# Two-layer hybrid trunk on eight cores: heads prepared evenly between the attention steps, and the output projection of the context block run inside the last pair of heads

## What is computed

```
u, cq_raw, ckv, krope = ab_split(h, w_in, kv_norm_g)
q = rms_norm(rms_norm(cq_raw) @ w_uq)            # 8 heads of 96, latent queries rotated
kv = ckv @ w_ukv                                 # k_nope 64 and v 64 per head
k = rms_norm(concat(k_nope, krope)); v
y_att = softmax(q k^T * 96**-0.5) v              # context: own 256 keys; latent: 512 cached + 1024 own
y = concat(y_pool, y_att) @ w_out                # 1024 x 1024
x = x + gate * y                                 # gate, shift, scale from silu(cond) @ ada_w + ada_b
x = x + gate2 * swiglu(norm(x))
```

## Time and profile before

| | |
|---|---|
| median of three runs | 1262.86 us |
| lowest, highest | 1261.05, 1441.05 us |
| profiled execution | 1259.46 us, span of its slowest core (5) 1258.4 us |
| spans of the eight cores | 1248.7 to 1258.4 us |
| mean granted clock of the cores | 0.955 to 0.972 |
| TensorE, VectorE, ScalarE, GpSimd busy | 90%, 38%, 34%, 18% of the span |
| preparation of pair 0 with pooling | 136.3 to 166.5 us |
| attention, four pairs | 166.5 to 359.6 us |
| output projection, to the first FFN matmul | 359.6 to 405.4 us |

### The profile page before, as it was taken

The page is one execution under the profiler, slowest core; times in us unless marked ns, Lnnn a source line. Parts: engine busy times, 40 slices in busy tenths (PEclk is TensorE's granted clock), DMA queues, the critical chain, the costliest instruction groups (busy, mean ns, idle before and its releaser), DMA issues.

```text
span 1258.4 us, 17871 instructions; the slowest of 8 cores (1248.7 to 1258.4 us)
## 1 busy us (share of the span) xinstructions
PE 1137.0 (90%) x6857; PEld 547.9 (44%) x6857; DVE 480.3 (38%) x814; ACT 429.5 (34%) x669; POOL 227.8 (18%) x347
## 2 busy tenths in 40 slices
PE   2477678797889899999999999998899999999998
PEld 1233455554544344444444444444344444444443
DVE  0355673634136211152252253565622225125133
ACT  2455466665745511101101156543651110110100
POOL 3311452533213200000000022224310000000000
PEclk9988997868799899999999999998999999999999
DMA  9960318778991425225224206003533321410013
GB/s 187 239 110 1 59 30 141 112 118 130 155 167 36 67 38 92 39 35 84 34 34 84 51 1 109 1 1 49 98 55 67 68 35 34 84 17 1 1 76 126
DMA packets 24977, 90.04 MB, mean 72 GB/s; under 512 B 3392, under 2 KB 3776, under 8 KB 24128
## 3 DMA queue, kind: packets, MB, share of 16 engines
q0 software_dynamic: 21312, 77.10, 36.8%
q1 hardware_dynamic: 3584, 11.80, 2.8%
HBM read 153.85 MB, written 6.88 MB: 128 GB/s over the span
## 4 chain that ended last, share of the span: by engine, by line
PE 76%; DVE 7%; DMA 6%; ACT 5%; POOL 3%; issue 3%; POOLq 0%; ACTq 0%; DVEq 0%
PE pb L230 74%; DMA wslot<-w_in_u 3%; DMA wslot<-ada_w 3%; ACT pt L247 2%; DVE xtmp L268 2%; PE pb L228 2%; DVE kT L274 1%; POOL qs L251 1%; DVE xb L268 1%; DVE qf L274 1%; POOL qr L251 1%; ACT hy L247 0%; ACT xsq L247 0%; POOL qt L251 0%; DVE utok L251 0%
## 5 line engine op out<-in xcount | busy, mean ns | idle before, releaser
L230 PE MATMUL pb<-hb,wslotx 128*128 128x512 bf16 x1440 | 319.9, 379 | 0.0
L247 ACT ACTIVATE sg<-pb 128x512 f32<-128x512 f32 x132 | 78.7, 596 | 472.0 <-PE pb L230 472.0
L251 DVE TENSOR_TENSOR apart<-pb,sg 128x512 bf16<-128x512 f32 x132 | 91.3, 691 | 369.0 <-PE pb L230 346.2
L230 PEld LDWEIGHTS pb<-hb,wslotx 128*128 128x128 bf16 x1440 | 140.8, 98 | 170.0 <-issue 0.3
L268 DVE SCALAR_TENSOR_TENSOR xb<-pb,mod,xb 128x512 f32<-128x512 f32 x192 | 143.6, 749 | 143.1 <-PE pb L230 143.1
L230 PE MATMUL pb<-hb,wslot 128*128 128x512 bf16 x864 | 197.6, 385 | 0.0
L230 PE MATMUL pb<-apart,wslot 128*128 128x512 bf16 x768 | 167.1, 379 | 0.0
L247 ACT ACTIVATE pt<-pb,rk 128x1024 bf16<-128x1024 f32 (+1 forms) x128 | 118.9, 953 | 58.0 <-PE pb L230 57.2
L230 PEld LDWEIGHTS pb<-hb,wslot 128*128 128x128 bf16 x864 | 85.6, 99 | 104.9 <-issue 5.7
L230 PEld LDWEIGHTS pb<-apart,wslot 128*128 128x128 bf16 x768 | 75.1, 98 | 90.2
L230 PE MATMUL pb<-hy,wslot 128*128 128x512 bf16 (+1 forms) x336 | 82.4, 397 | 4.7 <-ACT hy L247 4.5
(11 more groups left out here) (130 smaller groups left out, 953.8 us busy)
## 6 DMA issues: line engine op xcount, KB each, us to landing
wslot<-ada_w POOLq DMA_DIRECT2D x48, 512.0 KB, 10.1
wslot<-ffn_wd POOLq DMA_DIRECT2D x16, 512.0 KB, 9.9
wslotx<-ffn_wu POOLq DMA_DIRECT2D x14, 512.0 KB, 10.6
wslotx<-ffn_wg POOLq DMA_DIRECT2D x12, 512.0 KB, 18.9
y<-xb SPq DMA_DIRECT2D x12, 512.0 KB, 2.7
wslot<-ffn_wg POOLq DMA_DIRECT2D x10, 512.0 KB, 7.4
xb<-x_in POOLq DMA_DIRECT2D x4, 1024.0 KB, 41.7
wslot<-ffn_wu POOLq DMA_DIRECT2D x8, 512.0 KB, 7.5
```

What stands on the lines that cost most here:

```text
L230: return self.op("pe", lambda g: g.matmul(out, lhsT, rhs, start=start, stop=stop), [lhsT, rhs], [out], inc=inc)
L247: return self.op("act", lambda g: g.activation(out=out, in_=in_, func=func, bias=bias, scale=scale), reads, [out])
L251: return self.op(e, lambda g: g.tensor_tensor(out=out, in0=in0, in1=in1, op=op), [in0, in1], [out])
```

## The change

1. `qkv` is written in units `q_unit`, `k_unit`, `v_unit`, `sums` and `krstd`, each followed by one yield. For pair 0 the order is as before; for pairs 1 to 3 q units alternate with k and v. `sums` comes two ticks after its k unit, both rotations of a block come after its second q unit.
2. Pair 0 is prepared by `together`: a pooling call for each call of `qkv`, and six adaLN pieces spread over the 18 calls.
3. In pairs 0 to 2 of attention `nxt[0]` is called 18 times over 25 steps, and 28 adaLN pieces are spread over the 84 steps. In pair 3 six adaLN pieces come in steps 0, 2, .., 10.
4. `out_ctx` computes block 0's output projection in quarters of two matmuls, 32 calls over steps 8 to 26 of pair 3, with all eight groups in bank 6; adaLN pieces and `spread` use bank 7 alone then. The later `proj_out` covers blocks 1 and 2, and the norm of block 0 is queued before it.
5. The entries of `wo` come before adaLN pieces 42 to 47. There are eleven slots at first instead of ten, and seven `wslotx` instead of eight. `ukv`, `uq0`, `uq1` are freed at the start of pair 3 instead of after attention.
6. Room for the slot: `xrs` has two buffers instead of three, `ckr_f` is dropped earlier, and `new` takes the smallest gap that fits.

```diff
-        slots = [new("wslot%d" % i, [128, 2048], BF16, high=(i >= 7)) for i in range(10)]
+        slots = [new("wslot%d" % i, [128, 2048], BF16, high=(i >= 8)) for i in range(11)]
...
-        ent_ada(8, 48)
+        ent_ada(8, 42)
         for i in range(4):
             ent(("wo", i), ab_w_out[i], 8, 256)
+        ent_ada(42, 48)
...
+            order = [("q", b, u) for b in range(3) for u in range(2)] + [(c, kb) for kb in (3, 0, 1, 2) for c in "kv"] if p == 0 else [("q", 0, 0), ("k", 3), ("q", 0, 1), ("v", 3), ("q", 1, 0), ("k", 0), ("q", 1, 1), ("v", 0),
+                     ("q", 2, 0), ("k", 1), ("q", 2, 1), ("v", 1), ("k", 2), ("v", 2)]
+            for kind, *arg in order:
+                {"q": q_unit, "k": k_unit, "v": v_unit}[kind](*arg)
                 yield 0.5
                 tick()
...
+        pool12 = pooling([1, 2], FB, 0.5, lambda o, i, sc: P.act(o, i, AF.Copy, scale=sc))
+        together(qkv(0, (0, 1, 2, 3, 4, 5)), 18, [(pool12, 18), (ada, 6)])
...
+        def out_ctx():
+
+            ps = P.banks[6]
+            for m in range(8):
+                wo = W.get(("wo", m // 2))
+                for kc in range(8):
+                    P.mm(ps[:], wo[:, kc, (m % 2) * 128:(m % 2 + 1) * 128], hy[0][:, kc, :], start=(kc == 0), stop=(kc == 7), inc=(kc == 7))
+                    if kc == 7:
+                        residual_update(ps, 0, 2, m, 0)
+                    if kc % 2 == 1:
+                        yield
...
+        for i, _ in enumerate(attention(before)):
+            n = i % 28
+            if i < 84:
+                for k in range((n + 1) * 18 // 25 - n * 18 // 25):
+                    next(nxt[0], None)
+                if (i + 1) * early // 84 > i * early // 84:
+                    next(ada, None)
+                continue
+            if n == 0:
+                SB = (7,)
+                for key in ("ukv", "uq0", "uq1"):
+                    W.done(key)
+            if n < 16 and n % 2 == 0:
+                next(ada, None)
+            if n >= 8:
+                for k in range((n - 7) * 32 // 19 - (n - 8) * 32 // 19):
+                    next(octx, None)
...
-        stage(proj_out("wo", lambda b, kc: hy[b][:, kc, :], 0), fill, norms, 0, 1, hbs)
+        norms[0, 1, 0] = N.gen(0, 1, 0, hbs[0])
+        fill.append(norms[0, 1, 0])
+        stage(proj_out("wo", lambda b, kc: hy[b][:, kc, :], 0, (1, 2)), fill, norms, 0, 1, hbs)
```

More of the change, by code:

```diff
@@ L624, in stage, with proj_out @@
                     debt = 0.0
-        def proj_out(keys, src, l):
-            for b in range(3):
+        def proj_out(keys, src, l, blocks=(0, 1, 2)):
+            for b in blocks:
                 for m in range(8):
@@ new lines, in q_unit @@
+            def q_unit(b, u):
+                if u == 0:
+                    qst[b] = (ssr.next(), ssr.next(), [])
+                ss, sr, qts = qst[b]
+                ps = P.bank(banks)
+                for i in range(2):
+                    t = 4 * b + 2 * u + i
+                    P.mmg(ps[:, i * 192:(i + 1) * 192], [(cqn[:, kc, t * 128:(t + 1) * 128], wuq[kc][:, p * 192:(p + 1) * 192]) for kc in range(3)])
+                qf = qfr.next()
+                qs = qsr.next()
+                qt = qtr.next()
+                qts.append((qf, qt))
+                P.cp("dve", qf[:].rearrange("p a d -> p (a d)"), ps[:, 0:384])
+                P.tt("pool", qs[:], qf[:], qf[:], ALU.mult)
+                later(1, functools.partial(reduce, ss, u, qs))
+                if u == 1:
+                    later(2, functools.partial(rnorm, ss, sr))
+                    for v in range(2):
+                        later(3 + v, functools.partial(rotate, b, v, qts[v][0], qts[v][1], sr))
+                    later(6, functools.partial(turn, b, [x[1] for x in qts]))
@@ L1207, in attention, with together @@
                 todo.popleft()[1]()
-        q0 = qkv(0, (0, 1, 2, 3, 4, 5))
-        weave(q0, collections.deque([pooling([1, 2], FB, 0.5, lambda o, i, sc: P.act(o, i, AF.Copy, scale=sc))]), flush=True)
+        ada = ada_gen()
+        def together(main, n, parts):
+            for i, _ in enumerate(main):
+                for g, k in parts:
+                    for _ in range((i + 1) * k // n - i * k // n):
+                        next(g, None)
+        pool12 = pooling([1, 2], FB, 0.5, lambda o, i, sc: P.act(o, i, AF.Copy, scale=sc))
+        together(qkv(0, (0, 1, 2, 3, 4, 5)), 18, [(pool12, 18), (ada, 6)])
+        drain(pool12)
         drop(*pbr.t)
+        ytk = Ring([new("ytk%d" % i, [128, 12, 128], BF16) for i in range(2)])
         kvq.append(new_kvq(1))
-        ytk = Ring([new("ytk%d" % i, [128, 12, 128], BF16) for i in range(2)])
-        ada = ada_gen()
         nxt = [iter(())]
@@ L1241, in build @@
         N = Norm()
-        W.more([new("wslotx%d" % i, [128, 2048], BF16) for i in range(8)])
+        W.more([new("wslotx%d" % i, [128, 2048], BF16) for i in range(7)])
         norms = {}
```

88 lines of the change are left out of this document (27 added, 61 removed).

## The result

The changed kernel took 1273.19 us (median of 6 runs) against 1260.99 us for the kernel before on the same chip: ratio 1.0088, interval 1.0075 to 1.0101. That is within 2%, but on the slow side, and outside the predicted range of 1234 to 1270. All kernels of this document lie within 2% of the one before, so I go by these intervals and by the stages. The profiled execution was 1271.42 us; its slowest core, core 1, spans 1270.4 us.

A forecast was written before the change was run, and what follows sets the result against it. It took waits in a fixed order and the low clock to bound the first three pairs, ScalarE the pure step, TensorE the projection. Terms -9 - 4 - 2 + 1 + 16 - 13.8 = -11.8 us gave a median about 1251, range 1234 to 1270.

The forecast's parts named there:

- the signs that I named: Pairs 0 to 2: 46 to 48 us each, waits for k's copy about half of 10.4, clock above 0.85 in second and third.
- Term 1: Pairs 0 to 2: spreading the preparation over 25 steps shortens TensorE's waits, -9 us, between 0 and 18.5 gained.
- Term 2: Pairs 0 to 2: fewer steps without units bring back granted clock, -4 us; at most 11 gained, +15 if it stays low.
- term 3: Six adaLN pieces move from pairs 0 to 2 (-2 us) into pair 0's preparation (+1); landings in attention no later.
- term 4: Last pair: block 0's projection adds 11.0 us, bank 6 4.5, adaLN landing 2, clock -1.5; sum +16, between +8 and +23.
- term 5: Output projection loses the same 64 matmuls, -13.8 us, with nothing new late for the FFN.
- The last pair eats it: Last pair: bank 6 waited for in every group (8.8 us), adaLN late (5), +25 instead of +16; median 1264, chance 0.27.
- last pair above 58 us: Last pair: the sign named in advance for the rival in which it costs +25 us instead of +16.
- The low clock: Pairs 0 to 2: filled steps run mostly at clock 0.5, +15 us there; median 1279, chance 0.13.
- Units without waits: Pairs 0 to 2: evenly filled steps run without waits, -28 us there, sum -30; median 1233, chance 0.17.

The follow-up runs named there:

- old_11: The kernel before with the eleventh weight slot alone, adaLN pieces 9 and 10 issued behind the band table; the slot alone was worth -2 us in pairs 0 to 2.
- old_11_prep6: old_11 with six adaLN pieces in the preparation of pair 0 and 28 in the 84 steps, old generator of the heads; preparation 33.5 us.
- even_only: The kernel before with the new, evenly spread generator of the heads, ten slots, no adaLN pieces in the preparation of pair 0; pairs 0 to 2 took 155.0 us.
- all_early: Changed kernel, adaLN 9 and 10 behind the band table, 42 to 47 before projection weights and consumed before the last pair; 1252.83, 1257.23, 1318.71, 1342.84 us.
- all_early_noctx: all_early with block 0's output projection put back behind attention; last pair and projection together 80.5 us against 81.5.
- both_noctx: Changed kernel, adaLN 9 and 10 behind the band table, 42 to 47 before projection weights, block 0 projected after attention; last pair and projection 90.7 us.
- even_11: even_only with the eleventh weight slot, adaLN pieces 9 and 10 held back behind the band table; pairs 0 to 2 took 139.1 us.
- prep10_dve: prep10 with the six GpSimd operations of a q unit and its rotation on VectorE; pairs 0 to 2 took 148.7 us against 140.2.
- prep10: all_early with block 0's projection alternating banks 6 and 7, and ten adaLN pieces instead of six in pair 0's preparation; 1244.24 us, ratio 0.9865.

## Why the prediction was wrong

**Pairs 0 to 2 (terms 1 to 3): the sum right, the reasons not.** Forecast -9 - 4 - 2 = -15, measured -18.3; the signs that I named came: pairs at 43.2 to 46.9 us on core 5 (46 to 48 named), TensorE's waits for k's copy 6.3 instead of 10.4 us, granted clock 0.93 and 1.00. That the sum came out is luck, since the two large terms were off in opposite ways. Term 1 took -9 from the waits. On core 5 TensorE stood for 155.9 - 129.0 = 26.9 us before and 134.8 - 108.4 = 26.4 after: what the waits for k lost, those for the exponential took. Of the kernel before, 166.5 to 322.4 us, a row that the earlier trace rows leaves out:

```profile
PE pb L228 <- ACT pt L247: 4.7, 12, 0.8
```

After, it is 11.5. On the median core the time without work fell by 5 us. Term 2 took -4 from the clock, at most -11. TensorE's busy time fell by 13.9 us on the median core and by 20.7 on core 5, and 2.5 of that are the six pieces: the clock gave 11 and 18 us. Core 5 had the lowest clock of the eight in these pairs before, 0.80 against a median of 0.84, so reading it alone made this part look larger than it is on the others.

Term 1 also said of the spread that nothing is added and only VectorE's hand-overs change. It moves the rotations in GpSimd's queue, past the loads, and alone it is worth nothing. The eleventh slot, which term 3 gave "no later" and no figure, is worth 9 us beside it with 28 pieces and 16 with 34. The six pieces, priced at 6 x 0.41 less what a step hides, were worth 4.4 to 11.2 us. Late loads are a part of that only where there are any: from old_11 to old_11_prep6, with no load wait in either, they were worth 4.4, and busy time fell by 5.7.

**Preparation and before (term 3): missed.** I took +1. The stages up to the first pair grew by 6.5 + 1.3 + 3.5 = 11.3 us. The band table was the sentence "landings should be no later" applied to attention alone; I did not look at what the slot does to the first 50 us of the queue. The 1.3 us goes with the slot (old_11 has it, even_only does not). Of the preparation, 3 us go with the new interleaving, one pooling call for each call of `qkv`: even_only has 33.1 against 30.2 with no piece in it, and old_11_prep6, with the old generator, this interleaving and six pieces, has 33.5. TensorE was busy 20.0 us in even_only's preparation against 18.1 with the same work, at a granted clock of 0.79 against 0.89 on the median core; why is open. The pieces cost 1.1 of the 3.5, as taken.

**Last pair (term 4): this is the step that failed.** The sum was +16, bound +8 to +23; measured +29.9. Its parts: matmuls less slack 11.0, and bank 6 4.5. all_early against all_early_noctx measures both: 48.2 - 34.9 = 13.3, of which 3.6 are the bank (forecast 15.5 for the two). The sum of these two was right to 2.2 us. "I take +2, between 0 and +5" for the landing of the adaLN pieces was the error: 13.9 us on the median core, 11.6 to 15.8 on all. I had put the piece fifth or sixth in line at 3.2 us and subtracted a lead of 10 us, which already makes 6 to 9, more than my bound of 5. The lead was not there either: the piece was wanted at 329.01 - 15.78 = 313.2, six microseconds after the burst began at 307.12, since the slots of ukv and uq come free no earlier. And the queue does not finish its loads one by one. Five loads at 3.2 us would have ended at 323.1, six, with that of 304.14 still under way, at 326.3; the piece came at 329.0. In the 21.9 us from 307.12 the DMA engines moved 158 GB/s (core 5), 3.5 MB or 6.6 loads, so the loads behind piece 42 moved together with it. The clock gave nothing back (-1.5 taken): TensorE's busy time in this pair rose by 15.4 us on the median core, and the 64 matmuls are 13.8 of it. With the landing wait taken off, the last pair would have been 67.4 - 13.9 = 53.5 us, within the 51 to 54 that I named; the clock and landing terms in that figure, -1.5 and +2, nearly cancel.

**Projection (term 5):** -13.8, measured -12.4. Right, and no stall for the FFN's weights.

**Sum by its own terms:** pairs -18.3 for -15, up to the first pair +11.3 for +1, last pair +29.9 for +16, projection -12.4 for -13.8. Of the 22 us between 1251 and 1273, 14 are the last pair (12 of them the landing) and 10 the start; the three pairs and the projection together take 2 back.

**The rivals.** "The last pair eats it" (1264) is the nearest and had the sign "last pair above 58 us" right, but its price for landings was 5 us and its other parts (8.8 for the bank) did not come. The low clock did not follow the units: 0.90 to 1.00 on core 5, 0.93 on the median core. Units without waits (1233): no, ScalarE's exponentials alone are waited for 13.2 us.

## What to carry to other kernels

A load's lateness is not its length: draw the queue that issues it, entry by entry, for the place where it is wanted, and count the loads ahead of it and the arithmetic that stands between the issues; a slot that frees a stream changes every load behind it from the first microsecond on. If a stage is made shorter or filled, move the loads' demand with it: here the three pairs left the DMA engines at a share of 0.56 to 0.73, and the last one needed ten loads inside it instead of six. And work moved into a stage pays only when that stage has the loads and the banks for it: the move of the 64 matmuls gained nothing until the adaLN pieces had left and the second bank was free. Before a gain is put down to shorter waits, split the stage into busy and idle time: here the idle time of the three pairs hardly changed on the core that was read.

## What the runs showed of the hardware that was not expected

TensorE's granted clock fell in the long wait and was back 10 us behind it. Windows of core 5 in the last pair of the kernel after, cut at the wait's end:

```profile
core 5: us, PE busy (x) PEld busy (x) DVE busy (x) ACT busy (x) POOL busy (x), PEclk, DMA share, GB/s
312.50:322.50 10.00, 0.74 (x15) 0.39 (x11) 1.28 (x5) 1.03 (x3) 0.53 (x1) 0.69 1.05 158
322.50:329.00 6.50, 0.00 (x0) 0.02 (x1) 0.00 (x0) 0.00 (x0) 0.00 (x0) 0.50 0.99 157
329.00:339.00 10.00, 8.15 (x104) 5.19 (x104) 2.72 (x10) 5.64 (x9) 1.58 (x3) 0.61 1.04 174
339.00:349.00 10.00, 8.18 (x112) 4.64 (x112) 1.30 (x5) 5.31 (x5) 3.70 (x7) 1.00 1.04 176
```

The clock fell to its low level (1.2 GHz) in the wait, which began at 313.2, and was granted 0.61 on average in the 10 us behind it. The Trainium skill, "TensorE: Matmul & The Clock Gate", Part 1: The HAM clock gate, says that the default state is throttled and sustained activity releases it; the rows of and after the wait agree with that. The earlier trace rows do not: there the engine was busy 9.99 of 10 us at 0.50. Nor do the windows of core 1 in both_noctx, whose TensorE waited for no load in its last pair (305.2 to 347.9 us):

```profile
305.20:315.20 10.00, 8.76 (x108) 5.29 (x105) 3.65 (x14) 5.68 (x11) 2.11 (x4) 0.56 1.05 177
315.20:325.20 10.00, 9.21 (x112) 5.46 (x112) 0.91 (x4) 5.78 (x7) 1.69 (x4) 0.50 1.03 163
325.20:335.20 10.00, 8.38 (x75) 3.38 (x72) 1.12 (x4) 8.35 (x8) 2.01 (x4) 0.74 1.06 169
```

The clock stayed low for longer here, without the wait, than behind it there. So the wait is not shown to have cost clock beyond its own length.

The granted clock was the largest single part of the gain in the three pairs (0.84 before, 0.93 after on the median core, 11 us of the 18), and kernels that differ only in a weight slot differ in it (even_only 0.84, even_11 0.93).

The same arithmetic is dearer in a stage than its own length when its engine is one that others wait for: up to six short operations a unit on VectorE instead of GpSimd made three pairs 8.5 us longer (prep10_dve against prep10), nearly all of it time in which TensorE stood, although VectorE had been busy for only 74 of 140 us in them (prep10, core 5).
